# Attention heads in pairs: probabilities normalised before the turn, values in column groups, outputs with features on partitions

## What is computed

```python
for l in range(2):                       # first block
    sh1, sc1, g1, sh2, sc2, g2 = split(silu(c) @ w_ada[l] + b_ada[l], 6)
    h = x * (1 + sc1) + sh1
    y = mixer_ab(h) if l == 0 else mixer_cd(h)
    x = layer_norm(ALPHA * x + (1 + g1) * y)
    x = layer_norm(ALPHA * x + (1 + g2) * swiglu(x * (1 + sc2) + sh2))
# mixer_ab: 4 differential heads, oa = (softmax(q1 k1) - lam * softmax(q2 k2)) @ va, va 128 wide,
#           then an rms norm per head; 8 dilated heads, 64 wide
# mixer_cd: 8 causal heads with a bias, 8 forgetting heads (bias from a cumulative log gate), 64 wide
for layer in range(2):                   # second block: SwiGLU, mixer, SwiGLU
    x = x + 0.5 * swiglu(rmsnorm(x))
    x = x + (even: SSD and S5 | odd: 8 chunk-band heads of softmax(q k + bias) @ v, and a pooling)(rmsnorm(x))
    x = x + 0.5 * swiglu(rmsnorm(x))
```

## Time and profile before

| | |
|---|---|
| median of 3 runs | 1725.16 us (1724.41 to 1727.71) |
| the profiled execution, span | 1725.4 us |
| PE busy | 1658.2 us (96%), 12336 instructions |
| DVE busy | 1137.1 us (66%) |
| ACT busy | 791.2 us (46%) |
| POOL busy | 233.9 us (14%) |
| DMA | 330.23 MB, 191 GB/s on average |

### The profile page before, as it was taken

One profiled execution on the slowest core, in us unless ns is written; L12 is line 12 of the kernel. 1 busy time (PEld: TensorE's weight loads), 2 busy tenths in 40 slices (PEclk: granted clock), 3 DMA queues, 4 the chain that ended last, 5 costly groups with the idle time before them and its releaser, 6 DMA issues.

```text
span 1725.4 us, 30270 instructions
## 1 busy us (share of the span) xinstructions
PE 1658.2 (96%) x12336; PEld 1523.0 (88%) x12336; DVE 1137.1 (66%) x1385; ACT 791.2 (46%) x959; POOL 233.9 (14%) x300
## 2 busy tenths in 40 slices
PE   3999899999999999999999999999999999999998
PEld 2998799988987999889998978999899999889997
DVE  7877887888677444675657886555655557555554
ACT  1655433346445343453445656343544345553433
POOL 3000100000000000068946200000000004000000
PEclk8999999999999999999999999999999999999999
DMA  9954778784644655455554424555465555335552
GB/s 320 360 199 166 250 278 315 274 288 135 217 171 150 198 190 189 155 160 194 178 187 147 148 100 154 194 180 185 154 212 170 194 179 174 112 127 194 184 194 82
DMA packets 221391, 330.23 MB, mean 191 GB/s; under 512 B 6311, under 2 KB 183048, under 8 KB 221310
## 3 DMA queue, kind: packets, MB, share of 16 engines
q1 hardware_dynamic: 206112, 276.91, 48.0%
q0 software_dynamic: 14800, 52.06, 8.6%
q10 hardware_dynamic: 398, 0.11, 0.0%
HBM read 327.97 MB, written 1.09 MB: 191 GB/s over the span
## 4 chain that ended last, share of the span: by engine, by line
PE 82%; DVE 8%; ACT 4%; DMA 3%; issue 2%; SPq 0%; ACTq 0%; DVEq 0%; POOL 0%
PE bank L2380 41%; PE bank L2422 23%; PE bank L2410 7%; DVE s_wL L1871 2%; ACT s_wH L1504 2%; DVE s_late L1889 1%; PE bank L2392 1%; DMA s_raw<-in_w_in_ab 1%; DMA s_mix<-in_w_ada 1%; PE bank L2538 1%; PE bank L2530 1%; PE bank L2529 1%; DMA s_late<-in_w_ada 1%; PE bank L2479 1%; DVE s_mix L2083 0%
## 5 line engine op out<-in xcount | busy, mean ns | idle before, releaser
L1871 DVE TENSOR_TENSOR s_wL<-s_raw,s_wH 128x2048 fp32r<-128x2048 f32 x254 | 586.4, 2313 | 306.8 <-ACT s_wH L1504 306.2
L2380 PE MATMUL bank<-s_hH,s_wH 128*128 128x256 f32 x2240 | 636.9, 284 | 10.5 <-DVE s_hL L1919 5.2
L2380 PE MATMUL bank<-s_hH,s_wL 128*128 128x256 f32 x2240 | 634.5, 283 | 0.0
L2380 PE MATMUL bank<-s_hL,s_wH 128*128 128x256 f32 x2240 | 634.5, 283 | 0.0
L1504 ACT ACTIVATE s_wH<-s_raw 128x2048 fp32r<-128x2048 f32 x254 | 484.2, 1907 | 153.5 <-PE bank L2422 115.5
L2380 PEld LDWEIGHTS bank<-s_hH,s_wH 128*128 128x128 f32 x2240 | 430.3, 192 | 15.9 <-issue 11.6
L2380 PEld LDWEIGHTS bank<-s_hL,s_wH 128*128 128x128 f32 x2240 | 430.4, 192 | 2.3 <-issue 0.2
L2380 PEld LDWEIGHTS bank<-s_hH,s_wL 128*128 128x128 f32 x2240 | 430.4, 192 | 0.0
L2422 PE MATMUL bank<-s_wH,s_aH 128*128 128x512 f32 x488 | 192.1, 394 | 2.4 <-DVE s_aL L2089 2.4
L2422 PE MATMUL bank<-s_wL,s_aH 128*128 128x512 f32 x488 | 191.2, 392 | 0.0
L2422 PE MATMUL bank<-s_wH,s_aL 128*128 128x512 f32 x488 | 190.4, 390 | 0.0
(11 more groups left out here) (456 smaller groups left out, 2130.6 us busy)
## 6 DMA issues: line engine op xcount, KB each, us to landing
s_raw<-in_w_ffn_in SPq DMA_DIRECT2D x44, 1024.0 KB, 5.8
s_raw<-in_ffn_w_gate SPq DMA_DIRECT2D x44, 1024.0 KB, 5.1
s_raw<-in_ffn_w_up SPq DMA_DIRECT2D x44, 1024.0 KB, 5.1
s_raw<-in_ffn_w_down SPq DMA_DIRECT2D x44, 1024.0 KB, 4.8
s_late<-in_w_ada POOLq DMA_DIRECT2D x20, 2048.0 KB, 10.2
s_raw<-in_w_ffn_out SPq DMA_DIRECT2D x22, 1024.0 KB, 5.0
s_raw<-in_w_in_ab SPq DMA_DIRECT2D x12, 1024.0 KB, 11.5
s_raw<-in_w_in_cd SPq DMA_DIRECT2D x12, 1024.0 KB, 6.3
```

The lines of the kernel that those rows point to most:

```text
L1871: TTn(wL[:, slot, :], raw[:, slot, :], wH[:, slot, :].bitcast(F32), ALU.subtract).then_inc(lo_ready, 1)
L2380: last = mm(dst[:, ft * T:ft * T + T], w, h[:, k, :], start=opens(name, ft, k, i), stop=(k == KC - 1 and i == 2), skip_group_check=True)
```

## The change

Heads go in pairs: 8 of ab, 8 of cd, 4 of odd. A pair has the span of two dense steps. Per pair:

- `pair_scores`: four products, the two heads (partitions 0 to 63 and 64 to 127) alternating, in banks 0 and 1 (in odd 4 and 5).
- `pair_maxima`, `pair_probs`: both heads, one buffer each.
- `pair_normalise` on DVE scales the probabilities in SBUF before the turn. For the first four pairs of ab, the two maps of a differential head, it adds them with their factors into one matrix.
- `pair_turn`: six transposes (three for those four pairs), and it waits until the pair before has been read out of its bank (`o_done`), since bank 3 (7 in odd) serves both.
- `pair_values`: the values are the stationary side, 64 columns a head, the two heads in the two column halves, so that the result has features on partitions. Of ab's first four pairs the form stays that of before, with one set of products per head.
- `pair_out` parks the result in `t32` (`PARKED`), or in `nat` for ab's first four; `pair_direct` rounds it straight to hH, and `lower_parked` and `lower_direct` make hL.

`turn_o` stays for ab's first two groups alone. In odd, scores(0) and the pooling's products move ahead of unit 6, and the idle matmuls go. The scratch `sq` moves from gate1 to qT, `pW` to gate1 or late.

```diff
...
+            def pair_scores(name, p, banks, forget=False):
+                heads = HEADS[name][2 * p:2 * p + 2]
+                if forget:
+                    for (_, _, _, _, _, oc), b in zip(heads, banks):
+                        h = (oc - 512) // HD
+                        pick = head_pick[:, h:h + 1].to_broadcast([8, P])
+                        mm(bank[b][:, 0:384], pick, F8H, start=True, stop=False, skip_group_check=True)
+                        mm(bank[b][:, 0:384], pick, F8L, start=False, stop=False, skip_group_check=True)
+                for lo, hi, keys in ((0, 128, P), (128, 384, T)):
+                    for (tile, base, _, _, _, _), b in zip(heads, banks):
+                        q, k = qT[base:base + HD, tile, :], kT[base:base + HD, tile, :]
+                        at = slice(0, P) if lo == 0 else slice(P, T)
+                        last = mm(bank[b][:, lo:hi], q[:, at], k[:, 0:keys], start=not forget, stop=True, skip_group_check=True)
+                last.then_inc(s_ready, 1)
+            def pair_turn(name, p, b0, b1):
+                G = PAIR0[name] + p
+                pe.wait_ge(p_ready, G + 1)
+                if p >= 1:
+                    pe.wait_ge(o_done, G)
+                if shared_values(name, p):
+                    for i in range(3):
+                        last = pe.transpose(bank[b0][:, i * P:i * P + P], sW[:, 0, i * P:i * P + P], ident[:])
+                    last.then_inc(pT_ready, 1)
+                    return
+                for m in range(2):
+                    for i in range(2):
+                        last = pe.transpose(bank[b0][:, T * m + i * P:T * m + i * P + P], sW[:, m, i * P:i * P + P], ident[:])
+                last.then_inc(pT_ready, 1)
+                for m in range(2):
+                    last = pe.transpose(bank[b1][:, m * P:m * P + P], sW[:, m, T:T + P], ident[:])
+                last.then_inc(pT_ready, 1)
+            def pair_values(name, p, b):
+                pe.wait_ge(pT_copied, copies(name, p + 1))
+                heads, (w0, w1), oz = HEADS[name][2 * p:2 * p + 2], pW[name], bank[b]
+                if shared_values(name, p):
+                    c = slice(heads[0][2], heads[0][2] + P)
+                    mm(oz[:, 0:P], w0[:, 0:P], v[:, 0, c], start=True, stop=True)
+                    mm(oz[:, P:T], w0[:, P:T], v[:, 0, c], start=True, stop=False)
+                    mm(oz[:, P:T], w0[:, T:T + P], v[:, 1, c], start=False, stop=True).then_inc(o_ready, 1)
+                    return
+                for m, (_, _, vc, _, _, _) in enumerate(heads):
+                    mm(oz[HD * m:HD * m + HD, 0:T], v[:, 0, vc:vc + HD], w0[:, T * m:T * m + T], start=True, stop=False, skip_group_check=True)
+                for m, (_, _, vc, _, _, _) in enumerate(heads):
+                    last = mm(oz[HD * m:HD * m + HD, P:T], v[:, 1, vc:vc + HD], w1[:, P * m:P * m + P], start=False, stop=True, skip_group_check=True)
+                last.then_inc(o_ready, 1)
+
...
+            def pair_probs(name, p):
+                for m in range(2):
+                    act_e.wait_ge(s_max, 2 * (PAIR0[name] + p) + m + 1)
+                    for tt, (lo, hi) in enumerate(((0, 128), (128, 384))):
+                        last = A(sW[:, m, lo:hi], sW[:, m, lo:hi], ACT.Exp, scale=-1.0, bias=mx[:, m, tt:tt + 1],
+                                 accum_out=sums[:, m, tt:tt + 1])
+                    last.then_inc(e_ready, 1)
+            def pair_copy(name, p, b0, b1):
+                if p >= 1:
+                    act_e.wait_ge(o_ready, PAIR0[name] + p)
+                act_e.wait_ge(pT_ready, copies(name, p) + 1)
+                w0, w1 = pW[name]
+                if shared_values(name, p):
+                    A(w0[:, 0:384], bank[b0][:, 0:384], ACT.Copy).then_inc(pT_copied, 1)
+                    return
+                A(w0[:, 0:512], bank[b0][:], ACT.Copy).then_inc(pT_copied, 1)
+                act_e.wait_ge(pT_ready, copies(name, p) + 2)
+                A(w1[:, 0:T], bank[b1][:, 0:T], ACT.Copy).then_inc(pT_copied, 1)
+            def pair_out(name, p, b):
+                act_e.wait_ge(o_ready, PAIR0[name] + p + 1)
+                if shared_values(name, p):
+                    A(nat[:, :, P * p:P * p + P], blocks(bank[b][:, 0:T]), ACT.Copy).then_inc(o_done, 1)
+                else:
+                    A(blocks(t32[:, PARKED[name][p], :]), backwards(bank[b][:, 0:T]), ACT.Copy).then_inc(o_done, 1)
+            def pair_direct(name, p, c, b):
+                act_e.wait_ge(o_ready, PAIR0[name] + p + 1)
+                return A(blocks(hH[:, c, :]), backwards(bank[b][:, 0:T]), ACT.Copy)
+
...
+            def pair_normalise(name, p):
+                dve.wait_ge(e_ready, 2 * (PAIR0[name] + p) + 2)
+                step(dve.reciprocal(rs[:, 0:2, :], sums[:, 0:2, :]))
+                shared = shared_values(name, p)
+                if shared:
+                    step(TS(rs[:, 1, :], rs[:, 1, :], neg_lam, None, ALU.mult))
+                for m in range(1 if shared else 2):
+                    for tt, (lo, hi) in enumerate(((0, 128), (128, 384))):
+                        last = TS(sW[:, m, lo:hi], sW[:, m, lo:hi], rs[:, m, tt:tt + 1], None, ALU.mult)
+                if shared:
+                    step(last)
+                    for tt, (lo, hi) in enumerate(((0, 128), (128, 384))):
+                        last = STT(sW[:, 0, lo:hi], sW[:, 1, lo:hi], rs[:, 1, tt:tt + 1], sW[:, 0, lo:hi], ALU.mult, ALU.add)
+                last.then_inc(p_ready, 1)
+
...
+                turn(5)
+                pe.wait_ge(proj_evac, u0 + 11 + EVAC0)
+                scores(6)
+                if (4, 0) in ADA_TURN[l]:
+                    ada_turn(*ADA_TURN[l][4, 0], 7)
+                pe.wait_ge(proj_evac, u0 + 12 + EVAC0)
+                out_half(0, 0)
+                values(5)
+                pe.wait_ge(ada_out[1 - l], (6, 10)[l])
+                out_half(0, 1)
+                turn(6)
+                scores(7)
+                out_half(1, 0)
+                values(6)
+                out_half(1, 1)
                 out_half(2, 0)
-                values(15)
+                turn(7)
                 out_half(2, 1, (0,))
+                values(7)
                 ada_turn(*ADA_LAST[l], 2)
-                turn_o(3)
                 out_half(2, 1, (1,))
                 out_half(3, 0)
...
+                pair_maxima(name, 6, (0, 1))
+                if (4, 0) in ADA_STEPS[l]:
+                    ada_some(*ADA_STEPS[l][4, 0])
+                split_py(n0 + 14)
+                pair_normalise(name, 6)
+                for i in (1, 2, 3):
+                    if (4, i) in ADA_STEPS[l]:
+                        ada_some(*ADA_STEPS[l][4, i])
+                    if i == 1:
+                        lower_parked(4 * TR[o] + 2, 4, 1, PARKED[name][4])
+                        lower_direct(5, 3).then_inc(tl_ready, 1)
+                        dve.wait_ge(tl_ready, 4 * TR[o] + 3)
+                        dve.sem_inc(o_done, 1)
+                        pair_maxima(name, 7, (0, 1))
+                    elif i == 2:
+                        split_py(n0 + 15)
+                        pair_normalise(name, 7)
+                dve.wait_ge(oh_ready, l + 1)
+                lower_direct(6, 3).then_inc(o_done, 1)
                 split_py(n0 + 16)
-                normalise(15)
-                lower_o(3)
+                dve.wait_ge(th_ready, 4 * TR[o] + 4)
+                lower_direct(7, 3).then_inc(tl_ready, 1)
...
+                pair_probs(name, 6)
+                ada_done(*ADA_DONE[l][4, 0], 7)
+                split_py(n0 + 14)
+                upper_parked(4, 1, False)
+                pair_direct(name, 5, 5, 3).then_inc(th_ready, 1)
+                pair_copy(name, 6, 2, 3)
+                pair_probs(name, 7)
+                pair_direct(name, 6, 6, 3).then_inc(oh_ready, 1)
+                split_py(n0 + 15)
+                pair_copy(name, 7, 2, 3)
+                pair_direct(name, 7, 7, 3).then_inc(th_ready, 1)
+                ada_done(*ADA_LAST[l], 2)
                 split_py(n0 + 16)
-                ada_done(*ADA_LAST[l], 2)
-                upper_o(3)
                 sqrt_table()
...
```

More of the change, by code:

```diff
@@ L247, in build_program, with copies, shared_values @@
         }
-        HEAD0 = {"ab": 0, "cd": 16, "odd": 32}
+        PAIR0 = {"ab": 0, "cd": 8, "odd": 16}
+        def copies(name, p):
+            return {"ab": p if p <= 4 else 2 * p - 4, "cd": 12 + 2 * p, "odd": 28 + 2 * p}[name]
+        def shared_values(name, p):
+            return name == "ab" and p < 4
+        PARKED = {"ab": {4: 2}, "cd": {p: p for p in range(5)}, "odd": {0: 0}}
         TURN_BANK = {n: (0, 1, 2, 3) if n in ("ff0", "ff1") else (2, 3, 6, 7) if n == "f2a" else (4, 5, 6, 7) for n in TR}
@@ L947, in turn_o, with scores @@
-            def turn_o(g):
-                pe.wait_ge(o_done, g0 + 4 * g + 4)
-                if g:
-                    pe.wait_ge(tl_ready, ready + 3)
```

(52 more changed lines are left out.)

534 lines of the change are left out of this document (207 added, 327 removed).

## The result

| | before | after |
|---|---|---|
| median | 1724.54 us (1723.56 to 1727.71, 13 runs) | 1728.7 us (1727.47 to 1730.66, 13 runs) |
| ratio | | 1.0019 (95%: 1.0012 to 1.0026) |
| the profiled execution, span | 1725.4 us | 1725.6 us |
| PE, DVE, ACT busy | 1658.2, 1137.1, 791.2 us | 1638.9, 1134.5, 792.1 us |

The change makes the kernel slower, by 3.3 us by the ratio and 4.2 by the medians. The forecast, 1721.8, was 3.6 us faster: the sign is wrong, though the time lies in the range.

What follows compares the result with a forecast made beforehand. It took PE work to bound the kernel (82% of the chain): work -35.1, old waits -3.9, new waits +26.9 and half clock +8.5 sum to -3.6, against 1725.4 giving 1721.8 us; range 1711 to 1736.

Steps and rivals of the forecast that it cites:

- the sign: Whole kernel: faster, 3.4 us below the median of 1725.16; chances 0.45 faster, 0.35 slower, 0.20 the same.
- The path and the saved work: PE holds 82% of the chain that ended last, so matmuls taken out shorten the run: PE work -35.1 us.
- Scores: 20 pairs: two heads' products nearly side by side, 0.90 us a pair instead of 1.70, -16.0 us.
- values: 16 pairs in ab, cd and odd: two heads in column halves, 1.42 to 0.81 us a pair, -9.8 us.
- weight loads (1.1): Values: column tiling disables Fast Weight Load; with none hidden a pair would take 1.1 us, the sum 4.6 higher.
- a sequence (1.5): Pair's scores strictly one after the other, 1.55 us with less start-up: term -3.0 us instead of -16.0.
- turned outputs: ab, cd and odd: 32 transposes of outputs go, 8 x 0.44, -3.5 us.
- The waits: PE's new waits, mostly first turns and last quarters: ab 13.1, cd 12.1, odd 1.7, +26.9 us; old waits go, -3.9.
- The clock: Half-clock stretches of 3.4 us after waits over 2.5 us, five counted at 1.7 each: +8.5 us.
- A (the clock stays high): Rival: the new waits bring no half-clock stretches; 1713.3 us, chance 0.24.
- B (no overlap of the scores): Rival: a pair's scores do not run side by side, +13.0 us less 2.5 of waits; 1732.3 us, chance 0.18.
- C (a wait at every dense turn): Rival: DVE's split ahead of normalising makes each of 12 turns wait 1.0 us, +12; 1733.8 us, chance 0.12.

Runs made afterwards that it cites:

- the last quarter alone: Changed kernel with only the last quarter of ab and cd in a new queue order on DVE and ACT; 1702.0 us, 0.9856 to the kernel before.

## Why the prediction was wrong

**The path and the saved work: right, 1.6 too large.** Scores take 0.86 a pair against 0.90 taken, values 0.81 against 0.81, and neither weight loads (1.1) nor a sequence (1.5) showed. On the restriction of column tiling in the Trainium skill, "TensorEngine Tiling (Array Packing)", the trace is as before: a pair's values take 0.81, so it does not bind here. The forecast's -35.1 holds the wait of 0.46 behind the idle matmuls of the earlier trace rows, so its work is -34.6. Measured are -33.0 (13.6 + 12.3 + 7.1). By lines of the timelines at full clock, scores fell by 17.1 (forecast 16.0), values by 13.1 (12.6), turned outputs by 3.4 (3.5), the 8-row products of the forgetting heads by 0.9 and the idle matmuls of odd by 1.2; the turns grew by 0.6, where a fall of 1.2 was forecast. These are 35.0. The dense and output products between them, whose number is the same, took 2.1 more; why, I did not find out.

**The waits: right in place, 2.6 too large in all.** Their sum changed by +19.9 (9.6 + 12.1 - 1.8) against +22.5 (26.9 - 3.9 - 0.46). One by one, measured and forecast: ab 2.2 and 2.0, 2.9 and 3.0, 2.4 and 4.3, 0.5 and 0.4, 3.2 and 3.4; cd 2.6 and 2.6, 5.0 and 5.2, 1.9 and 0.5, 3.8 and 3.8; odd 1.1 and 1.7. (For turn(6) of ab the forecast's own terms, 11.3 against 6.7, give 4.6.) It waits less because PE reaches it late: the halves before it lay in a stretch at half clock. In the profile with unit 16's split last that stretch is missing, and turn(6) waits 3.99.

**The clock: the step that failed.** I took one stretch of 3.4 us for each wait over 2.5 us and dropped one: five, 8.5 us. There were eight new ones, 13.6 us, of which 12.6 fall outside the waits: 4.1 more than forecast. The wait of 5.04 had three around it, beginning inside it (503.4 to 513.7), and the one of 1.94 at 523 had one, while those of 2.43 and 2.60 had none. The rule came from one profile (the page's slices, 43 us long, can't show a stretch of 3.4), and the others don't keep it. The wait of 2.38 near 207 was followed by a stretch in 7 of 11 profiles, that of 2.0 at the start of cd in 3 of 10, and that of 2.6 at cd's first turn in 3 of 5 (not in the changed kernel's profile, nor in that of the last quarter alone). So a wait of some 2 us may or may not bring a stretch. Filling the waits gave back 12.1 us, so the term is real.

From -3.6 to the +0.2 between the profiles: work +1.6, waits -2.6, new stretches +4.1, the start's half clock +0.9, the time ahead of ab and all the rest -0.3 (0.1 is lost in rounding). The waits' error hid part of the clock's.

**The rivals.** A (the clock stays high) is refuted by the profile, and the run with idle matmuls shows what it would have given. B (no overlap of the scores) is refuted by 0.86 and by the run in one row half, which landed at the price it would have had. C (a wait at every dense turn) did not come: pairs 1 to 5 wait 0.24 at most. The change was slower by the forecast's own mechanism. The net of -3.6 was the difference of terms of 39 and 35 us, so the error of 4.1 in the clock alone turns its sign.

What stays open: the medians differ by 3.3 to 4.2 us, the two profiles by 0.2, so about half of what the forecast missed is in neither profile. The forecast compared the span of 1725.4 with the median of 1725.16 as if they were the same quantity; with the 1.9 between them that execution was 2.1 slower than that median, and nothing here shows what made it so. Executions of either kernel differ by 3 to 4 us, and I have only one profile of each. Which waits bring the clock down was not settled either.

## What to carry to other kernels

When work on the bound engine is cut by making its partners' steps longer and serial, write down for each new wait what stands in the partner's queue ahead of the instruction that releases it, and move what isn't due yet behind it: here the same instructions in another order were worth 34 us, ten times the net effect of the change. Give a bank back (read it out) before starting the next long job on the reading engine. Count a wait of PE of 2 us or more at its length and 1.7 us more for each 3.4 us stretch of half clock that may follow it: none, one or, with the 5 us wait, three here. Don't take the number from one profile. Where a wait can't be removed, idle matmuls in it kept the clock up. Before comparing two profiles, see where each execution stands among the others of its kernel.

## What the hardware showed that I had not expected

- Products in the two row halves overlap whatever their order: 0.86 us for a pair alternating, 0.87 one head after the other, 1.50 when both use rows 0 to 63.
- A long wait has stretches at half clock inside it, not only after it: 5.04 us of waiting up to 505.07, and 10.2 us of half clock from 503.4 on. Only what lies outside the wait costs time.
- Behind the start the stretches are 3.4 us long or two to four times that, in all eleven profiles, and cost half their length; idle matmuls of 0.25 us in the waits removed seven of eight.
- A trace may have no record of the clock at its start, and the view then prints 1.00: up to 49.4 us the products of the changed kernel start 0.21 us apart, as they do at a granted 0.50.
